# Moving the rounded operands of TensorE to other byte offsets of SBUF in a hybrid DeltaNet and MoBA block

## The reference, cut to what matters

```python
def hybrid_layer(x, ...):                      # x: 1 x 256 x 1024, float32
    h = rms_norm(x, norm_pre_w)
    proj = jnp.einsum('bsd,df->bsf', h, w_in)  # 1024 x 10256
    ...                                        # split: q, k, v of both mixers, gates
    oa = gated_delta_rule(qa, ka, va, g, beta)             # 8 heads of 128
    ya = rms_norm(oa, dn_onorm_w) * jax.nn.silu(z_a)
    ob = moba_attention(heads_b(qb), heads_b(kb), heads_b(vb), rel_bias)
    yb = ob * jax.nn.silu(z_b)
    gates = jax.nn.sigmoid(gate_logits + b_gate).reshape(bsz, s, 2, d)
    pa = jnp.einsum('bsf,fd->bsd', ya, w_branch[0])
    pb = jnp.einsum('bsf,fd->bsd', yb, w_branch[1])
    merged = gates[:, :, 0] * pa + gates[:, :, 1] * pb
    out = jnp.einsum('bsd,de->bse', merged, w_out)
    return x + rms_norm(out, norm_post_w)
```

## The kernel before, in words

| tensor | bytes of a partition | start | start modulo 2048 | modulo 256 |
|---|---|---|---|---|
| `raw`, `w_hi`, `w_lo` | 16384 each | 16512, 32896, 49280 | 128 | 128 |
| `xin`, `cst` | 8192, 1536 | 65664, 73856 | 128 | 128 |
| `h_hi`, `h_lo` | 8192 each | 77632, 85824 | 1856 | 64 |
| `acc`, `kT_all`, `act`, `bT` | 2048 to 8192 | 104896 and on | 448 | 192 |
| `sub` | 10240 | 173568 | 1536 | 0 |
| `y_hi`, `y_lo` | 16384 each | 193088, 209472 | 576 | 64 |

## Time and profile before

### The profile page before, as it was taken

How to read it: one execution, slowest core, us unless ns; L and a number is a source line. 1 busy time by engine, 2 the same in 40 slices (tenths; PEclk the granted TensorE clock), 3 DMA queues, 4 the chain that set the end, 5 groups by cost and what they waited for, 6 DMA issues and landing times.

```text
span 355.8 us, 6674 instructions
## 1 busy us (share of the span) xinstructions
PE 347.6 (98%) x2387; PEld 318.4 (89%) x2387; DVE 270.0 (76%) x551; ACT 218.8 (62%) x483; POOL 58.7 (16%) x114
## 2 busy tenths in 40 slices
PE   7999999999999999999999999999999999999993
PEld 5889998888899999999999999999998888888882
DVE  3869897599997868978788797878977656566744
ACT  5877894542457667686867766777676544425421
POOL 1534436500050000301103020030301101000011
PEclk9999999999999999999999999999999999999999
DMA  8667948793698485446745565465534735766423
GB/s 264 178 193 194 334 158 270 198 329 119 167 257 228 121 214 141 121 122 164 188 120 128 145 178 147 120 164 145 165 121 138 247 118 172 254 226 236 124 113 118
DMA packets 76206, 63.48 MB, mean 178 GB/s; under 512 B 4724, under 2 KB 62478, under 8 KB 76174
## 3 DMA queue, kind: packets, MB, share of 16 engines
q1 hardware_dynamic: 73838, 59.37, 57.3%
q0 software_dynamic: 1152, 3.30, 3.1%
q10 hardware_dynamic: 1184, 0.39, 0.5%
HBM read 61.46 MB, written 1.59 MB: 177 GB/s over the span
## 4 chain that ended last, share of the span: by engine, by line
PE 84%; DVE 8%; DMA 3%; issue 2%; ACT 1%; POOL 0%; DVEq 0%; SPq 0%; ACTq 0%; POOLq 0%
PE banks L1395 40%; PE banks L1450 15%; PE banks L1657 6%; PE banks L1413 6%; DVE w_lo L919 3%; DVE sub L1061 2%; DMA xin<-in_x_dram 1%; DMA raw<-in_w_in_dram 1%; DMA sub<-m_blocks 1%; PE banks L1545 1%; PE banks L1523 1%; PE banks L1562 1%; PE banks L1551 1%; PE banks L1380 1%; DVE sub L1063 1%
## 5 line engine op out<-in xcount | busy, mean ns | idle before, releaser
L919 DVE TENSOR_TENSOR w_lo<-raw,w_hi 128x1024 fp32r<-128x1024 f32 x102 | 123.8, 1220 | 42.3 <-ACT w_hi L670 41.6
L670 ACT CAST w_hi<-raw 128x1024 fp32r<-128x1024 f32 x103 | 107.2, 1047 | 30.0 <-PE banks L1450 12.3
L1395 PE MATMUL banks<-h_hi,w_hi 128*128 128x256 f32 x440 | 64.0, 288 | 0.2 <-DVE acc L989 0.2
L1395 PE MATMUL banks<-h_lo,w_hi 128*128 128x256 f32 x440 | 59.4, 277 | 0.0
L1395 PE MATMUL banks<-h_hi,w_lo 128*128 128x256 f32 x440 | 59.3, 277 | 0.0
L1395 PEld LDWEIGHTS banks<-h_hi,w_hi 128*128 128x128 f32 x440 | 55.2, 189 | 0.7 <-DVE acc L989 0.3
L1395 PEld LDWEIGHTS banks<-h_hi,w_lo 128*128 128x128 f32 x440 | 54.2, 188 | 0.0
L1395 PEld LDWEIGHTS banks<-h_lo,w_hi 128*128 128x128 f32 x440 | 54.2, 188 | 0.0
L989 DVE SCALAR_TENSOR_TENSOR acc<-banks,vec,acc 128x255 f32<-128x255 f32 (+2 forms) x72 | 34.5, 480 | 3.7 <-ACT acc L790 1.5
L616 POOL TENSOR_TENSOR so<-so,rnq 128x2 f32<-128x2 f32 x8 | 2.0, 251 | 162.8 <-ACT junk L857 162.8
L790 ACT ACTIVATE acc<-banks,vec 128x256 f32<-128x256 f32 x16 | 7.6, 473 | 17.4 <-PE banks L1395 17.4
(11 more groups left out here) (258 smaller groups left out, 607.6 us busy)
## 6 DMA issues: line engine op xcount, KB each, us to landing
raw<-in_w_in_dram SPq DMA_DIRECT2D x80, 512.0 KB, 4.9
raw<-in_w_branch_dram SPq DMA_DIRECT2D x16, 512.0 KB, 4.7
raw<-in_w_out_dram SPq DMA_DIRECT2D x8, 512.0 KB, 4.2
xin<-in_x_dram SPq DMA_DIRECT2D x2, 512.0 KB, 3.8
th_E<-g_rows POOLq DMA_DIRECT2D x2, 512.0 KB, 7.2
bias<-bias_rows POOLq DMA_DIRECT2D x1, 1024.0 KB, 7.5
raw<-in_x_dram SPq DMA_DIRECT2D x2, 512.0 KB, 3.7
out_dram<-xin SPq DMA_DIRECT2D x4, 256.0 KB, 2.0
```

Of the source, the lines that this page charges most:

```text
L670: nc.scalar.copy(w_hi[:, t % SLOTS, :], raw[:, t % SLOTS, :]).then_inc(s_hi, 1)
L919: v.tensor_tensor(w_lo[:, t % SLOTS, cols], raw[:, t % SLOTS, cols], w_hi[:, t % SLOTS, cols].bitcast(F32), ALU.subtract).then_inc(s_lo, 1)
L1395: last = mm(ps, w, r, start=part == 0 and k == 0, stop=part == 2 and k == KT - 1)
```

## The change

Only the order of the declarations changes, and so the start bytes. Sizes, instructions, queues and semaphores are the same.

```diff
+        gt = sb("gt", [P, 12, NC, HEADS])
+        wbd2 = sb("wbd2", [P, KT, 4 * HEADS], F32R)
+        ssqk = sb("ssqk", [P, NC, HEADS])
+        ng = sb("ng", [P, NC, HEADS])
         raw = sb("raw", [P, SLOTS, D])
         w_hi = sb("w_hi", [P, SLOTS, D], F32R)
         w_lo = sb("w_lo", [P, SLOTS, D], F32R)
+        bd = sb("bd", [P, NC, 2 * HEADS])
+        h_hi = sb("h_hi", [P, KT, SEQ], F32R)
+        h_lo = sb("h_lo", [P, KT, SEQ], F32R)
+        y_hi = sb("y_hi", [P, 2, HEADS, SEQ], F32R)
+        y_lo = sb("y_lo", [P, 2, HEADS, SEQ], F32R)
         xin = sb("xin", [P, NC, D])
...
-        wbd2 = sb("wbd2", [P, KT, 4 * HEADS], F32R)
...
-        h_hi = sb("h_hi", [P, KT, SEQ], F32R)
-        h_lo = sb("h_lo", [P, KT, SEQ], F32R)
...
-        bd = sb("bd", [P, NC, 2 * HEADS])
-        gt = sb("gt", [P, 12, NC, HEADS])
...
-        ng = sb("ng", [P, NC, HEADS])
...
-        ssqk = sb("ssqk", [P, NC, HEADS])
...
-        y_hi = sb("y_hi", [P, 2, HEADS, SEQ], F32R)
-        y_lo = sb("y_lo", [P, 2, HEADS, SEQ], F32R)
```

## The result

The changed kernel takes 364.63 us (364.47 to 364.85), the kernel before in the same comparison 357.52 (357.46 to 357.59): a ratio of 1.0199, 95% interval 1.0183 to 1.0214, or 7.1 us more. The forecast was 351.9 us, the range 346.5 to 360.0.

A forecast was written before the change was run, and what follows sets the result against it. TensorE's float32r streams were taken as the bound; the weights' move gains 5.6 us and all else nothing, so 355.8 - 5.6 = 350.2 us of span, with 1.75 around it 351.9 us; range 346.5 to 360.0.

The forecast's parts named there:

- What bounds the kernel: Whole span: TensorE, busy 98% at full clock; in 64 to 106 us VectorE's chain covers it.
- The stall per matmul: float32r streams: 4 ns lost with 256 columns, 13 ns with 512, against 109 and 216 ns.
- The stall is not the weight load's: float32r matmuls: 32 stationary columns take 114.4 ns, no less than 128, so the weight load was excluded as cause.
- The weights at a boundary of 2048 bytes: w_hi, w_lo moving with 512 columns, 128 to 0: 432 matmuls gain 0 to 5.6 us, upper end taken.
- `h` from 64 to 128: h_hi, h_lo moving with 256 columns, 1320 matmuls: -5.3 to +2.0 us, no change taken.
- The distance modulo 256: Rival, all float32r streams: starts 128 apart in every pair end both stalls, 10.9 us gained, 346.6 us; 20%.
- Slower: Rival, h streams: phase 128 modulo 256 is slow, 1320 matmuls at 114.5 ns, 359.5 to 362.0 us; 20%.
- Its stronger half: Head tiles of L1395: TensorE kept in the 2.83 us rhythm, 0.09 us on some 50 tiles, +4.5, 362.0 us.
- The cover of the 64 to 106 us stretch: 12 gate tiles there: VectorE's chain covers them, a faster TensorE only waits for the splits; nothing counted.
- Nothing happens: Rival, float32r streams: stall is the price of four bytes a cycle or of the array, 357.5 us; 27%.
- The loads: Transfers into raw, now begun at a multiple of 256 bytes: 0 to 1 us gained, nothing taken.
- The share of the first stretch in the gain: First of the three stretches not covered by VectorE: TensorE loses 1.1 us of its time.

The follow-up runs named there:

- The fourteen kernels of the table: The kernel before, the changed kernel and twelve kernels with other start bytes of weights, h and y; 357.5 to 366.81 us.
- The narrow thirds: L1395's third of h_lo by w_hi with 32 of 128 stationary columns: in the changed kernel 362.46 us, in the kernel before 357.44 us.
- w0_h64: Changed kernel with h back at 1856 modulo 2048 and y at 64 modulo 256, weights staying at 0: 363.16 us, ratio 1.016.
- w0_h192: Changed kernel with h and y at 192, weights staying at 0, so the old distance 192 from other starts: 358.24 us, ratio 1.0011.
- w0_h0: Changed kernel with h and y at 0 like the weights, distance 0: 363.10 us, ratio 1.0157.
- w128_h128: Changed kernel with the weights back at 128 and h, y staying at 128, distance 0: 363.52 us, ratio 1.0168.

## Why the prediction was wrong, step by step

- What bounds the kernel: right. All of the 7.1 us are TensorE's pace in the float32r streams; the splits stand at 1217 and 1046 ns, the pace of the plain float32 pieces is as before.
- The stall per matmul, 4 and 13 ns above 109 and 216: right as a measure of today's excess, wrong as a measure of what alignment could give. The fourteen kernels of the table, at ten distances, have no pace below 114.3 and 227.7 on average. Of the 13 ns at 512 columns placement gave back 1.4; of the 4 ns at 256 none.
- "The stall is not the weight load's": the step that failed. The row set a short load in one stream against a long one in another, at the places of the kernel before, and a short and a long load cost the same at distance 192 also if the reads miss each other there. I took "costs nothing at this place" for "costs nothing", and so held the load out of the sum. The narrow thirds show it: 113.6 and 113.9 ns before, 114.7 and 119.0 after. The row held a hint too: its stationary slices lie 128 bytes apart (by the declared sizes they begin at 128 and 0 modulo 256), so half of its matmuls stand at distance 192 and half at 64, where a full load later took 117.6 ns (w0_h64).
- The weights at a boundary of 2048 bytes, 0 to 5.6 us gained, upper end taken: wrong in its ground. No start byte counts by itself (w0_h192 against before, w0_h0 against w128_h128). The term of 5.6 us gained was a loss: +3.4 ns for each 512-column matmul by the long pieces, 3.7 by the table, and 576 of them are 2.0 to 2.1 us.
- `h` from 64 to 128, no change taken, bounds -5.3 to +2.0 us: the size was off as well. It is +4.4 ns for each of 1320 matmuls, 5.8 us, nearly three times the upper bound. That bound was the pace of today's `w`, chosen for its start byte; the nearer row was the tile of 2.83 us, the other rhythm of the same work. The two losses together are 7.8 to 7.9 us, more than the 7.1 measured, since TensorE waits less after the change (the point on the cover, below).
- The distance modulo 256 stood among the rivals, with the right mechanism and the wrong sign: I put the new 128 down as the distance at which both stalls go. No row of the trace before had another distance in these two forms, so the sign was open, and a stream that stands at one point of 256 bytes could be on the best or on the worst. It stood on the best.
- "Slower": the side was right, the ground (the start of `h`) was not, and 359.5 to 362.0 was too small. Its stronger half, all head tiles in the rhythm of 2.83 us, is nearly what happened (2.85); what it lacked is the loss on 512 columns.
- The cover of the 64 to 106 us stretch was put at more than it is. In the kernel before TensorE has no gap in the 144 matmuls of L1450, and waits for some 0.6 us in all, between 101 and 107 us; after the change these waits are gone. So a loss per matmul passes through but for 0.6 us. Whether a gain would have been held back no run shows. Of the 1.54 us at the first mark 0.9 had come before the first matmul of L1450 (64.27 and 65.17 us).
- "Nothing happens", 357.5 us, which the prediction drew from the rows and set beside the Trainium skill, "SBUF — State Buffer", sections "Specifications (TRN2)" and "Who interferes with whom": the time moved by 2%, so lines of 16 bytes and independent ports do not tell the cost of these streams.
- The loads were put at nothing: their median from issue to landing is 4.8 us, where it was 4.9. The share of the first stretch in the gain was 96 x 13 ns, 1.2 us and not 1.1; the sum does not hang on it.

## What to carry to other kernels

When TensorE streams float32r operands back to back, the placement of the two operands relative to each other was a cost of up to 2.5% here that no dependency shows; measure the pace (piece of the chain by number of matmuls) for a few relative offsets in steps of 16 or 32 bytes before a layout is changed for neatness, and then keep the relative offset with padding when tensors are moved. A row that shows a resource to be free tells it for its own configuration only: where a change alters that configuration, the row bounds nothing.

## What was not expected of the hardware

- The pace of the two forms depends on the operands' distance modulo 256, and 16 bytes matter: 114 to 120 ns with 256 columns, 227.7 to 234 with 512. At one distance other start bytes changed it by 0.8 ns at most (114.3 and 115.1 at 192).
- The two forms want different distances, 192 and 0; `h` at 192 is the better compromise, since 256 columns are more frequent here.
- At one layout there are two rhythms for the same tile, 2.74 and 2.83 us, and a tile can stay in the slower one to its end. At distance 192 from other starts more tiles take the slow one (10 of 44 against 3 of 45). What selects it stays open, as does why single distances are fast, and where the remaining 4 and 12 ns above 109 and 216 go.
